# Earlier loading of one expert's gate and up weights, and another queue for the item table, in a hybrid attention and mixture-of-experts layer

## What is computed

```
logits = (hf @ w_router) + b_router
top_val, top_idx = lax.top_k(logits, TOP_K)          # 4 of 32
gates = jax.nn.softmax(top_val, axis=-1)
...
def expert_block(args):
    xb, e = args
    gu = xb @ w_gate_up[e] + b_gate_up[e]             # 1024 -> 2048
    gate, up = gu[:, :D_EXPERT], gu[:, D_EXPERT:]
    gate = jnp.minimum(gate, SWIGLU_LIMIT)
    up = jnp.clip(up, -SWIGLU_LIMIT, SWIGLU_LIMIT)
    act = (up + 1.0) * gate * jax.nn.sigmoid(SWIGLU_ALPHA * gate)
    return act @ w_down[e] + b_down[e]                # 1024 -> 1024
```

## Time and profile before

| | |
|---|---|
| median of 3 runs | 2413.63 us (2413.55 to 2413.87) |
| the profiled execution's own time | 2407.64 us |
| its span, first to last instruction | 2406.0 us |
| PE busy | 2365.7 us, 98% of the span |
| mean granted TensorE clock | 0.997 of full |
| DVE, ACT, POOL busy | 55%, 19%, 18% |

### The profile page before, as it was taken

How to read it: one execution, slowest core, us unless ns; L and a number is a source line. 1 busy time by engine, 2 the same in 40 slices (tenths; PEclk the granted TensorE clock), 3 DMA queues, 4 the chain that set the end, 5 groups by cost and what they waited for, 6 DMA issues and landing times. The chain is left out here.

```text
span 2406.0 us, 45416 instructions
## 1 busy us (share of the span) xinstructions
PE 2365.7 (98%) x15707; PEld 1612.7 (67%) x15707; DVE 1333.8 (55%) x2479; ACT 459.0 (19%) x1148; POOL 422.2 (18%) x589
## 2 busy tenths in 40 slices
PE   8999999999998999999999999999999999999999
PEld 6765664444444888888888888888656565655544
DVE  4665674111356554455445554556767676776565
ACT  3434552000022100000000000100212222121332
POOL 2451102121243310001100111110110101011230
PEclk9999999999999999999999999999999999999999
DMA  5000002312052898888888888888999899999462
GB/s 151 27 18 10 1 0 53 122 26 52 27 178 88 271 378 319 284 293 293 288 301 307 286 300 314 302 305 324 329 337 356 325 359 339 343 346 338 160 201 88
DMA packets 255034, 531.84 MB, mean 221 GB/s; under 512 B 17846, under 2 KB 67910, under 8 KB 254951
## 3 DMA queue, kind: packets, MB, share of 16 engines
q1 hardware_dynamic: 222302, 472.57, 55.4%
q0 software_dynamic: 17440, 38.97, 5.2%
q10 hardware_dynamic: 15208, 19.14, 2.2%
HBM read 498.76 MB, written 31.87 MB: 221 GB/s over the span
## 5 line engine op out<-in xcount | busy, mean ns | idle before, releaser
L1937 PE MATMUL banks<-arena_a,arena_w 128*128 128x144 f32 (+7 forms) x4608 | 568.4, 286 | 2.2 <-ACT arena_a L2109 2.2
L1937 PEld LDWEIGHTS banks<-arena_a,arena_w 128*128 128x128 f32 x4608 | 564.6, 190 | 9.0 <-issue 6.5
L1990 PE MATMUL banks<-arena_w,arena_a 128*64 128x256 f32 x2688 | 298.6, 380 | 3.0 <-DVE arena_a L2268 1.7
L1990 PEld LDWEIGHTS banks<-arena_w,arena_a 128*64 128x64 f32 x2688 | 193.3, 137 | 107.2 <-issue 14.1
L2363 DVE TENSOR_SCALAR arena_m<-banks,arena_m 128x160 f32<-128x160 f32 x144 | 55.3, 384 | 302.8 <-PE banks L1937 302.3
L2164 ACT ACTIVATE arena_m<-arena_m 128x160 f32<-128x160 f32 x144 | 48.5, 337 | 789.0 <-DVE arena_m L2363 474.3
L1305 POOL DMA_DIRECT2D arena_m<-slot_tokens x32 | 18.7, 585 | 1026.6 <-issue 1026.6
L1945 PE MATMUL banks<-arena_w,arena_a 128*64 128x256 f32 x1728 | 197.5, 381 | 0.0
L2046 PE MATMUL banks<-arena_w,arena_a 128*128 128x512 f32 x448 | 194.6, 592 | 0.0
L1945 PEld LDWEIGHTS banks<-arena_w,arena_a 128*64 128x64 f32 x1728 | 120.9, 137 | 67.6 <-issue 10.4
L2046 PEld LDWEIGHTS banks<-arena_w,arena_a 128*128 128x128 f32 x448 | 84.0, 190 | 100.4 <-issue 100.4
(11 more groups left out here) (411 smaller groups left out, 3440.9 us busy)
## 6 DMA issues: line engine op xcount, KB each, us to landing
arena_w<-in_w_gate_up_dram SPq DMA_DIRECT2D x128, 2048.0 KB, 12.7
arena_w<-in_w_down_dram SPq DMA_DIRECT2D x32, 4096.0 KB
expert_rows<-arena_a ACTq DMA_DIRECT2D x104, 128.0 KB, 9.3
arena_a<-in_x_dram SPq DMA_DIRECT2D x16, 512.0 KB, 4.9
arena_w<-in_w_in_dram SPq DMA_DIRECT2D x16, 512.0 KB, 5.4
arena_a<-in_b_down_dram SPq DMA_DIRECT2D x14, 512.0 KB, 15.3
expert_rows<-arena_a ACTq DMA_DIRECT2D x28, 192.0 KB
arena_a<-in_b_down_dram SPq DMA_DIRECT2D x72, 64.0 KB
```

The lines of the kernel that those rows point to most:

```text
L1937: m = pe.matmul(GU[f % 3][:, to:to + width], w[c][:, k, at:at + P], xT[:, k, 0:width], start=(k == 0), stop=(k == K - 1), skip_group_check ...
L1990: m = pe.matmul(at[h * TH:(h + 1) * TH, :], x[:, k, :], w[:, k, h * QB:(h + 1) * QB], start=(start and k == 0), stop=(stop and k == KH - 1 ...
```

## The change

Three edits. First, chunk 1 of expert 0's gate and up is loaded in three pieces: the gate half (2 MB) and the first half of up (1 MB) by SP during the last pair of routing, once product 5 of that pair is made (the gate half lies where `w1` was, which product 5 reads, the first half of up where `w2` was, which product 6 reads before it, the second half of up where `w4` is, which the last product reads); the second half of up (1 MB) where the whole chunk was. As three transfers of 16 counts each signal it, the waits for chunk 1 ask for 48 in place of 32. Second, the item table's two transfers are issued by ACT, after it has copied item 0's rows and before its first sigmoid; SP goes on to `load_down(0)` without waiting for the table. Third, in the tail of routing there are 30 identity transposes before `ranks` of the last tile in place of 10, and 10 behind it.

```
@@ route, sync
                 for n in range(T):
                     b = n % 2
                     rows = slice(tile_of(n) * P, (tile_of(n) + 1) * P)
+                    if n == T - 2:
+                        sp.wait_ge(out_done, made(PAIRS - 1, 5))
+                        sp.dma_start(wg[1], gate_second).then_inc(w_gu_here[1], 16)
+                        sp.dma_start(wu[1][:, 0:KH, :], up_second[:, 0:KH, :]).then_inc(w_gu_here[1], 16)
                     sp.wait_ge(sem("x1_sum"), n + 1)
...
                 sp.wait_ge(out_done, 7 * PAIRS)
                 sp.wait_ge(rows_here, 32)
-                load_gate_up(sp, 0, 1)
+                sp.dma_start(wu[1][:, KH:K, :], up_second[:, KH:K, :]).then_inc(w_gu_here[1], 16)
@@ route, tensor
                 logits(T - 1)
+                stay_warm(WARM * 3 // 4)
+                ranks(T - 1)
                 stay_warm(WARM // 4)
-                ranks(T - 1)
@@ experts, sync
-                sp.wait_ge(sem("fields"), 1)
-                sp.dma_start(item_dram, fields_i[0:ITEM_ROWS, :]).then_inc(sem("table"), 16)
-                sp.wait_ge(sem("table"), 16)
-                sp.dma_start(items[:, :], item_dram.rearrange("(o i) f -> o (i f)", o=1)).then_inc(sem("table"), 16)
                 load_down(sp, 0)
                 load_bias(0)
                 sp.wait_ge(sem("table"), 32)
@@ experts, tensor (and two more places)
-                            wait_value(pe, w_gu_here[c], 32 * i + 32)
+                            wait_value(pe, w_gu_here[c], 32 * i + (32 + 16 * c))
@@ experts, scalar
                 keep_x(0)
+                act.wait_ge(sem("fields"), 1)
+                act.dma_start(item_dram, fields_i[0:ITEM_ROWS, :]).then_inc(sem("table"), 16)
+                act.wait_ge(sem("table"), 16)
+                act.dma_start(items[:, :], item_dram.rearrange("(o i) f -> o (i f)", o=1)).then_inc(sem("table"), 16)
                 expert_item(0)
```

More of the change, by code:

```diff
@@ L1287, in load_gate_up @@
                 eng.dma_start(w[c], w_gate_up[bass.ds(e, 1)][:, :, at:at + CW].rearrange("o (k p) n -> p (o k) n", p=P)).then_inc(w_gu_here[c], 16)
+        gate_second, up_second = (w_gate_up[0][:, at:at + CW].rearrange("(k p) n -> p k n", p=P) for at in (CW, FF + CW))
         def load_down(eng, e):
@@ L2271, in sum_w1 @@
                     b11, b12, b21, b22 = quarters(c)
-                    wait_value(dve, w_gu_here[c], 32 * i + 32)
+                    wait_value(dve, w_gu_here[c], 32 * i + (32 + 16 * c))
                     if c:
```

## The result

| | median of the runs, us | lowest to highest | profiled execution (span) |
|---|---|---|---|
| before | 2412.59 (20 runs) | 2408.32 to 2414.77 | 2407.64 (2406.0) |
| after | 2415.86 (20 runs) | 2412.48 to 2418.94 | 2418.25 (2416.6) |

The ratio after to before is 1.0014, 95% interval 1.0008 to 1.0020: the change makes the kernel slower by 3.3 us. I had predicted 2410.3 with a range up to 2414.4, so both the time and the direction were wrong.

What follows compares the result with a forecast made beforehand. It took PE, busy 98%, as the bound; the first two terms vanish into the wait for item 1's gather, which comes 3.3 us earlier, giving 2410.3 us. Range: 2407.4 to 2414.4 us.

Steps and rivals of the forecast that it cites:

- What bounds the kernel: Whole kernel: PE busy 98%, never waiting for chunk 1; around the change three holes of 2.58, 2.23 and 2.95 us.
- First term: Routing's tail: added transposes keep the clock full, so PE starts on item 0's gathered rows 1.1 us earlier.
- The sum: At item 1's start: PE goes on at 827.7 in place of 830.95, 3.3 us gained, giving 2410.3 us.
- A: PE's start on item 0's gathered rows: about 786.7 instead of 787.80, 1.1 us gained, at least 0.
- rival 3: Early 3 MB load slows POOL's scatters; first gather starts at 788, not 782.2; kernel at 2416.6 us; chance 0.07.
- Second term: Start of item 0's gate and up: the half clock from 792 to 795.5 may vanish, 1.7 or 0 us, even odds.
- Third term: Item 1's gather: table's first transfer lands at 808.5, later reads and gathers save 3.0 us, gather there at 827.7.
- rival 1: Table passes fast, landing at 801, and the clock holds: 5.8 us gained, 2407.9 us; chance 0.23 of 5 us or more.
- rival 2: Table lands only at 812 when SP's queue is dry, PE stops 1 to 3 us; about 2413.6 us; chance 0.20.
- the two unfavourable cases: rival 2, a late table (about 2413.6 us, chance 0.20), and rival 3, a late first gather (2416.6 us, chance 0.07).

Runs made afterwards that it cites:

- the control: The kernel before, unchanged, run and profiled again on the second chip: 2412.75 us against 2412.52, ratio 1.0003.
- e2: The kernel before with only the item table moved to ACT's queue: 2415.72 us against 2410.01 for before, ratio 1.0026.
- e3: The kernel before with only the identity transposes regrouped (30 ahead of the last tile's counts, 10 behind): 2410.07 us against 2410.01, ratio 0.9998.
- e8: e7 with POOL's waits for the last routing scatters put behind the first two gathers: 2406.68 us against 2412.52 for before, ratio 0.9981.
- e7: The kernel after with the table back on SP's queue (pieces and transposes kept): 2410.75 us against 2412.52 for before, ratio 0.9994.
- e9: The kernel after, with SP issuing the down weights only once the table's first transfer has landed: 2405.32 us against 2407.04 for before, ratio 0.9991.
- e6: The kernel after, unchanged, run again on the second chip: 2418.63 us against 2412.52 for before, ratio 1.0029.
- e4: The kernel after with 64 table rows written instead of 59, to spread over 16 engines: 2413.21 us against 2410.01 for before, ratio 1.0016.
- e11: e8 with 70 identity transposes instead of 44 behind the two small matmuls: 2409.24 us against 2407.04 for before, ratio 1.0008.
- e1: The kernel before with only chunk 1's three pieces and the waits for 48: 2410.72 us against 2410.01 for before, ratio 1.0000.
- e12: e8 run again on the third chip: 2406.30 us against 2407.04 for before, ratio 0.9997.

## Why the prediction was wrong, step by step

**What bounds the kernel.** "PE never waits for chunk 1" and "the first edit removes no wait" were read off one execution, and do not hold for the kernel: the control waits 3.4 us there, e2 4.7 and e3 4.3. I should have asked by how much chunk 1 was in time. The earlier trace rows already showed it at 117 GB/s just before it was due, and the shown execution lay 6.0 us below the median, which I only carried over as an offset. That offset may in part be this wait; no run shows by how much.

**First term (1.1 us).** Its clock part was right: the thirty transposes took 3.47 us, the 44 took 5.00 and L1540 took 0.61, all at the full granted clock, where before the clock was at half from 778.4. Transposes alone did hold it, which speaks against the section on PE-mode transpose in the Trainium skill's "TensorE: Matmul & The Clock Gate", that they don't count as busy; e3 agrees with after (granted clock 1.00 from 776 to 790 and on to 811). But the term presumed a gather at 781.8, and it came at 790.47. The sum's A was 1.1 us gained; in the profiled pair it was 7.8 us lost. This was rival 3, the late scatter, to which I had given 0.07. My argument against it, "3 MB at 396 GB/s are in by 759", took a rate from a stretch without scatters. Here the ten microseconds from 750 moved 232 GB/s (windows of after: length, busy of five engines, granted clock, DMA share, GB/s):

```profile
750.00:760.00 10.00, 10.00 (x44) 4.38 (x42) 7.18 (x24) 0.76 (x2) 4.39 (x4) 1.00 0.90 232
...
788.80:802.50 13.70, 5.92 (x23) 5.52 (x24) 12.19 (x42) 1.70 (x4) 9.62 (x11) 0.50 0.56 169
...
840.00:843.40 3.40, 2.96 (x14) 2.44 (x16) 0.00 (x0) 1.12 (x3) 0.00 (x0) 0.52 1.00 347
```

That the 3 MB slow the scatters is in all the traces: from the start of the first of the three to the start of the third POOL took 25.9 to 30.7 us in the nine with the early pieces, 21.8 to 24.0 in the five without. That the wait for the scatter then holds the gather is shown by e8 against e7, where only that wait moved. In the one trace of the third chip that has this wait (e9) it did not hold the gather, so the loss is not the same in each execution. What the prediction missed altogether is that the table is made behind the same scatter (`dst_free`).

**Second term (even odds of 1.7 us).** It had the wrong sign. In the idle stretch of 9.0 us that the late gather makes, the granted clock falls to half, 1.2 GHz, and stays there through 5.9 us of PE's work, worth 3.0 us; behind the second hole it is down for another 3.0 us of PE's work, worth 1.5, as the last two rows above show. In the kernel before, PE worked 3.4 us at half clock at this place, worth 1.7 (it had had a stretch ahead of it, at the transposes).

**Third term, which carried the sum (3.3 us gained).** This is the step that failed: the landing of the table's first transfer at 808.5. In after it landed at 821.50, 13.0 us later. 7.2 of these are its issue: I took "about 797" as given, and it was 804.29, since the late scatter held DVE. The other 5.8 are the transfer, for which I took 11.4 us on ACT's queue; it took 17.2, 17.6 and 19.1 us in after, e2 and e6. e2, whose table was issued on time (796.24), shows that the transfer alone turns the gain into a loss. I had reckoned 1.5 us to the first packet and 59 turns of 0.2 us. The turns were right: in e2 these are the packets from 812.0 to 812.6 us, 61 of down weights on sixteen engines, so about four on each, and four of the table on its one:

```profile
q1 hardware_dynamic: 61, 0.25, 101.9%
q10 hardware_dynamic: 4, 0.00, 0.5%
```

One for one, and the 60 took about 10 us, near the 11.8 of the sum. (The Trainium skill's "DMA: Bandwidth & Descriptors", section on queues, rings and completion order, has 9 to 17 descriptors taken before a switch; no such run of the table's rows is seen here, and rival 1, for which it spoke, did not occur.) What was missing is the time before: with SP's queue full no packet of the table moves for 7 to 9 us (6.7 in after, about 7 in e4, 8 in e2, 9 in e6). I had 1.5 us, for which the prediction has no row. With the down weights held back, in e9, all 60 packets lie between 800.8 and 801.5 us, 0.6 to 1.3 us behind the issue:

```profile
q10 hardware_dynamic: 60, 0.00, 5.8%
```

On the kernel's side three things hang on the landing, and all moved. ACT's wait, which I had let off up to 809.2 or 810.9, passed its slack (step 5 could have begun at 822.7, which less my 3.0 us allows a landing by 819.7) and stopped PE 2.0 us (3.97 in e6); item 1's gather came late, a hole of 2.4 us, though PE went on 18.9 us behind the landing in after and e6, close to my 19.2; SP's load of item 1's gate and up went out at 823.76 in place of 815.19; PE never waits for it. The down weights were as I had expected in time: DVE's L2377 reads them at 827.54 without waiting. That is rival 2's mechanism, beyond its bound: I had the table land by 812 at the latest, "SP's queue is dry". That bound was wrongly summed: at the chunk's pace (4 MB from 787.03 to about 807.6) the 5.4 MB take 27.7 us and not 25. That pace was right, since SP's load was issued at 795.64 and the down weights landed at 823.3 (27.2 us behind 796.07); but the start was 8.6 us late, by the late gather.

**The sum and the chances.** The table costs 5.7 us by e2 and 7.9 by e6 against e7. The pieces and transposes together give 1.8 us by e7, inside its interval. -1.8 and +7.9 make the 6.1 us of the second chip, by construction; the first measurement has 3.3. I had left 0.05 for slower by more than 0.2% and put 2414.4 as the upper end, because the two unfavourable cases, a late table and a late gather, were priced one at a time. They have one cause, weights moved beside small transfers, and came together, the late scatter making the table late as well.

**Left open.** Why a new queue's first packet needs 7 to 9 us when another is full, whether POOL's scatters have a part in it, and why the scatters and the weights slow each other down, is observed and not explained. So is the difference between the second and the third chip (the version of e8 is worth 5.8 us on one and 0.7 on the other), and e11's idle stretch.

## What to carry to other kernels

A small transfer that several engines wait for gains nothing by a queue of its own if a bulk load is issued beside it: what counts is what is under way on the engines when it is issued, and the cheap cure here was one wait that holds the bulk load back (17.2 us in after, 5.2 in e9). A bulk load moved forward must be priced at the places of all small transfers beside which it now runs, and where the next consumer stands behind a wait for one of these that it doesn't need, that wait should be moved first. Before saying that a wait is absent, look at how much margin its arrival had, and whether the profiled execution is a typical one.

## What was not expected of the hardware

- A table of 59 rows of 52 bytes on a queue of its own moved no packet for 6.7 us (after), about 8 (e2) and 9 (e6), and one of 64 rows none for 7 us (e4), while the other queue had 4 MB or more and POOL's scatters were moving for most of the time; alone, all its packets had gone 1.3 us after the issue, and the landing was seen 3.9 us later still (801.5 to 805.44 in e9).
- A 3 MB load beside one tile's scatter made that scatter's landing 10.8 us instead of 4.7, in e1 8.9, in e7 10.1; in e11 and e12 that one took 5.9 and 6.1, and the next 8.5 and 8.3. The ten microseconds of the load moved 232 GB/s in after.
- Identity transposes kept the granted clock at 1.00 from 775.84 to 786.60 in after, 10.8 us with only a few small matmuls among them; e3 is alike.
